# Where head outputs, norms and modulation stand in a two-block transformer kernel with hand-written engine programs

## Time and profile before

| | us |
|---|---|
| runs | 2436.47, 2440.69, 2446.38 |
| median of the runs | 2440.69 |
| profiled execution | 2446.27 |
| its span | 2444.5 |
| TensorE matmuls, busy | 1869.2 (76%) |
| TensorE weight loads, busy | 1217.9 (50%) |
| VectorE, busy | 813.5 (33%) |
| ScalarE, busy | 519.2 (21%) |
| GpSimd, busy | 87.7 (4%) |

### The profile page before, as it was taken

How to read it: one execution, slowest core, us unless ns; L and a number is a source line. 1 busy time by engine, 2 the same in 40 slices (tenths; PEclk the granted TensorE clock), 3 DMA queues, 4 the chain that set the end, 5 groups by cost and what they waited for, 6 DMA issues and landing times.

```text
span 2444.5 us, 28941 instructions
## 1 busy us (share of the span) xinstructions
PE 1869.2 (76%) x12708; PEld 1217.9 (50%) x12708; DVE 813.5 (33%) x1269; ACT 519.2 (21%) x776; POOL 87.7 (4%) x140
## 2 busy tenths in 40 slices
PE   7989999999998999787766666666566666666665
PEld 7879899988787998776321111211121211122111
DVE  5645567766455667554100110011001100110012
ACT  5625433345344343332000000000000000000000
POOL 1200000011000000010000000000000000000000
PEclk9999999999999999867977876888788877887886
DMA  7334557663345677324999999999999999999996
GB/s 242 96 127 150 179 175 258 207 193 121 121 138 164 207 249 240 122 112 198 390 429 429 429 429 428 429 429 429 429 429 430 429 429 429 428 429 428 430 429 265
DMA packets 171068, 739.79 MB, mean 303 GB/s; under 512 B 6672, under 2 KB 133136, under 8 KB 146240
## 3 DMA queue, kind: packets, MB, share of 16 engines
q1 hardware_dynamic: 168592, 731.27, 75.2%
q0 software_dynamic: 2352, 6.69, 0.8%
HBM read 736.88 MB, written 1.05 MB: 302 GB/s over the span
## 4 chain that ended last, share of the span: by engine, by line
DMA 47%; PE 40%; DVE 7%; ACT 4%; issue 2%; POOL 0%; SPq 0%; DVEq 0%; ACTq 0%
PE PS L325 39%; DMA WB<-in_w_down 24%; DMA WB<-in_w_up 23%; DVE WL L1430 2%; ACT WH L953 2%; DMA W<-in_w_in 1%; DVE X L1425 1%; DVE C L1425 1%; DVE S L1425 1%; DVE C L1422 0%; DMA W<-in_w_ck 0%; DVE S L1497 0%; DVE T L1422 0%; ACT S L983 0%; ACT C L1318 0%
## 5 line engine op out<-in xcount | busy, mean ns | idle before, releaser
L325 PE MATMUL PS<-WB,XS 128*32 128x352 f32 x3072 | 365.2, 637 | 210.1 <-DMA WB<-in_w_up 122.6
L325 PE MATMUL PS<-WB,S 128*32 128x512 f32 x1408 | 269.6, 762 | 152.1 <-issue 77.7
L1430 DVE TENSOR_TENSOR WL<-W,WH 128x2048 fp32r<-128x2048 f32 x141 | 323.4, 2294 | 169.0 <-ACT WH L953 169.0
L325 PEld LDWEIGHTS PS<-WB,XS 128*32 128x32 f32 x3072 | 115.9, 141 | 456.8 <-issue 178.9
L1425 DVE SCALAR_TENSOR_TENSOR S<-S,PS 128x352 f32<-128x352 f32 (+1 forms) x110 | 63.3, 588 | 792.9 <-ACT S L1395 756.2
L325 PE MATMUL PS<-HTh,WH 128*128 128x256 f32 x1064 | 307.0, 289 | 8.4 <-DVE WL L1430 4.7
L953 ACT ACTIVATE WH<-W 128x2048 fp32r<-128x2048 f32 x141 | 269.0, 1908 | 205.0 <-PE PS L325 190.6
L325 PE MATMUL PS<-HTl,WH 128*128 128x256 f32 x1064 | 302.4, 284 | 0.0
L325 PE MATMUL PS<-HTh,WL 128*128 128x256 f32 x1064 | 302.2, 284 | 0.0
L325 PEld LDWEIGHTS PS<-WB,S 128*32 128x32 f32 x1408 | 71.7, 128 | 339.7 <-issue 224.7
L325 PEld LDWEIGHTS PS<-HTh,WH 128*128 128x128 f32 x1064 | 205.0, 193 | 10.6 <-DVE WL L1430 5.2
(11 more groups left out here) (261 smaller groups left out, 2114.2 us busy)
## 6 DMA issues: line engine op xcount, KB each, us to landing
WB<-in_w_down SPq DMA_DIRECT2D x64, 2816.0 KB, 36.1
WB<-in_w_gate SPq DMA_DIRECT2D x48, 2816.0 KB, 35.9
WB<-in_w_up SPq DMA_DIRECT2D x48, 2816.0 KB, 35.9
C<-in_w_gate SPq DMA_DIRECT2D x16, 2816.0 KB, 36.5
C<-in_w_up SPq DMA_DIRECT2D x16, 2816.0 KB, 37.6
W<-in_w_in SPq DMA_DIRECT2D x31, 1024.0 KB, 6.7
S<-in_w_ada SPq DMA_DIRECT2D x24, 1024.0 KB, 5.3
W<-in_w_gate SPq DMA_DIRECT2D x22, 1024.0 KB, 7.9
```

The costliest lines, as they stand in the source:

```text
L325: return e.matmul(o, l, r, start=start, stop=stop, skip_group_check=True)
L1430: e.tensor_tensor(M.WL[i][:, :], M.W[:, 2048 * (m % NW):2048 * (m % NW) + 2048], M.WH[i][:, :].bitcast(F32), ALU.subtract).then_inc(*up("l ...
```

## The change

- **Head outputs**: scores are always in bank 0, transposed probabilities in bank 1, the output c in bank 2 + c % 2, with a signal `o_out` for its emptying; they draw no rotating bank. The first unit of `w_out` waits for each of the four banks as it comes to it (`of=("heads", l)`). `ret_s(0)` and `ret_s(1)` come before `heads(9)`, on VectorE `decayed(0)` and `decayed(1)` too.
- **Retention**: VectorE takes the first step of `retained()` (the sums) before the next unit's low part, not behind it. Six empty steps stand ahead of the split of the turned rows.
- **Modulation**: `modulation(12l)` is made in the cross attention, `modulation(12l + n + 1)` and `ada_sum(12l + n)` in slot n, the last sum before `down(10)`; the loads are put two slots earlier into the order of units.
- **Norms**: the squares are scaled by 1/32, so that the mean is one operation. VectorE scales the first half of the rows' columns, ScalarE the second, into `XN1` (exp: `XE`; mem, gm and at in place). TensorE turns by plain transposes. `pre_norm` turns all chunks of t = 0 before those of t = 1. A place with fewer than two fill units uses `pre_norm` behind them. exp's `XP` is made from `XE`, behind the evictions, by both engines. In a post-norm the first product comes ahead of the mean.

```diff
 
-    def turning(name, srcs, chunks, by=None, eighths=False):
-
+    def turning(name, srcs, chunks):
         for k0 in range(0, chunks, 2):
             ps = two(take(("turn", name, k0)))
             for k in range(2):
                 for t in range(2):
                     o, i = ps[:, k, 128 * t:128 * t + 128], srcs[t][:, 128 * (k0 + k):128 * (k0 + k) + 128]
-                    if eighths:
-                        i = srcs[t].rearrange("p (q k) -> p k q", k=8)[:, k0 + k, :]
-                    ins = e.transpose(o, i, M.ID) if by is None else mm(o, i, by[:, 128 * t:128 * t + 128], True, True)
+                    ins = e.transpose(o, i, M.ID)
             ins.then_inc(*up("full", "turn", name, k0))
             yield
 
...
-    def norming(name, src=X, dg=M.DG, eighths=False):
+    def norming(name, rows=M.XN1):
         yield
-        e.wait_ge(*at("diag", name))
-        yield from turning(name, [src[:, 0, :], src[:, 1, :]], 8, dg, eighths)
+        e.wait_ge(*at("scaled_first", name, 1))
+        e.wait_ge(*at("scaled_second", name, 1))
+        yield from turning(name, [rows[:, 0, :], rows[:, 1, :]], 8)
 
     def pre_norm(name, eighths=False):
-        for _ in norming(name, eighths=eighths):
-            pass
+
+
+        for t in range(2):
+            e.wait_ge(*at("scaled_first", name, t))
+            for k0 in range(0, 8, 2):
+                use = ("turn", name, k0)
+                if eighths or k0 == 4:
+                    e.wait_ge(*at("scaled_second", name, t))
+                if t == 0:
+                    take(use, hold=True)
+                ps = two(PS[:, 4 + C.banks.uses[use][0], :])
+                for k in range(k0, k0 + 2):
+                    i = M.XE[:, t, :].rearrange("p (q k) -> p k q", k=8)[:, k, :] if eighths else M.XN1[:, t, 128 * k:128 * k + 128]
+                    ins = e.transpose(ps[:, k - k0, 128 * t:128 * t + 128], i, M.ID)
+                if t:
+                    ins.then_inc(*up("full", *use))
+                    drop(use)
 
...
-        nrm = norming(name)
-        next(nrm)
         if len(units) < 2:
             for u in units:
                 fill(layer, *u)
-            for _ in nrm:
-                pass
+            pre_norm(name)
             return
+        nrm = norming(name)
+        next(nrm)
...
 
         def scores(h):
             c, po = h // 2, 64 * (h % 2)
-            ps = PS[:, h % 2, :]
-            if h >= 2:
-                e.wait_ge(*at("sc_out", l, h - 2))
+            ps = PS[:, 0, :]
...
 
         def values(h):
             c, po, Q = h // 2, 64 * (h % 2), M.PQ[h % 2]
-            ps = PS[:, 4 + C.banks.held[("o", l, c)], :] if h % 2 else take(("o", l, c), hold=True)
+            ps = PS[:, 2 + c % 2, :]
+            if h % 2 == 0 and c >= 2:
+                e.wait_ge(*at("o_out", l, c - 2))
+            elif h % 2 == 0 and l:
+                e.wait_ge(*at("yfree", "ffn", l - 1, 1, c))
             e.wait_ge(*at("pt_out", l, h))
             if h % 4 == 0:
                 e.wait_ge(*free("vv", l, h // 4))
             mm(ps[po:po + 64, 0:256], M.V[:, 0, 64 * h:64 * h + 64], Q[:, 0:256], True, False)
             mm(ps[po:po + 64, 128:256], M.V[:, 1, 64 * h:64 * h + 64], Q[:, 256:384], False, True).then_inc(*up("pv", l, h))
-            if h % 2:
...
             for _ in turning((w, l), [src[:, 0, :], src[:, 1, :]], 2):
                 pass
         fill(l, *f1)
-        heads(9)
         ret_s(0)
         ret_s(1)
+        heads(9)
         y = ("mix", l)
-        e.wait_ge(*free("o", l, 1))
-        for h in range(6, 8):
-            e.wait_ge(*at("sc_out", l, h))
-            e.wait_ge(*at("pt_out", l, h))
-        out_unit("w_out", l, 1, y, start=True)
+        e.wait_ge(*at("o_out", l, 1))
+        e.wait_ge(*at("sc_out", l, 7))
+        e.wait_ge(*at("pt_out", l, 7))
+        out_unit("w_out", l, 1, y, of=("heads", l), start=True)
         beside.finish(rec)
         psY = two(take(("ry", l), hold=True))
         ret_v(0)
         ret_v(1)
         ret_s(2)
         ret_s(3)
-        e.wait_ge(*free("o", l, 3))
+        e.wait_ge(*at("o_out", l, 3))
         out_unit("w_out", l, 2, y)
...
                 values(i - 2)
+            if i in (1, 2):
+                C.units.order.append(("ada", 12 * l + i - 1))
         e.wait_ge(*free("co", l, 2))
...
-            if n > 1:
-                ada_sum(12 * l + n - 2)
+            ada_sum(12 * l + n)
             proj_t("w_up", l, n, HT, ("u", l, n))
             if n > 1:
                 down(n - 2)
-            C.units.order.append(("ada", 12 * l + n))
+            if n < 10:
+                C.units.order.append(("ada", 12 * l + n + 2))
         down(9)
-        ada_sum(12 * l + 9)
+        ada_sum(12 * l + 11)
         down(10)
-        C.units.order.append(("ada", 12 * l + 11))
-        ada_sum(12 * l + 10)
-        ada_sum(12 * l + 11)
 
...
 
-    def squares(name, src, junk, ready):
+    def squares(name, src, ready):
         for t in range(2):
             for h in range(2):
                 e.wait_ge(*at(*ready, t, h))
-                e.activation(junk[t][:, 512 * h:512 * h + 512], src[:, t, 512 * h:512 * h + 512], ACT.Square,
+                e.activation(M.XN1[:, t, 512 * h:512 * h + 512], src[:, t, 512 * h:512 * h + 512], ACT.Square, scale=1.0 / 32,
                              accum_out=K["ss4"][:, 2 * t + h:2 * t + h + 1]).then_inc(*up("sq", name, t, h))
+
+    def scaled(name, src=X, dst=M.XN1):
+
+        for t in range(2):
+            e.wait_ge(*at("rstd", name, t))
+            e.activation(dst[:, t, 512:1024], src[:, t, 512:1024], ACT.Copy, scale=K["rs"][:, t:t + 1]).then_inc(
+                *up("scaled_second", name, t))
...
                 e.wait_ge(*at("pv", l, h - 2))
-            e.activation(M.PQ[h % 2][:, 0:384], PS[:, 2 + h % 2, 0:384], ACT.Copy).then_inc(*up("pt_out", l, h))
+            e.activation(M.PQ[h % 2][:, 0:384], PS[:, 1, 0:384], ACT.Copy).then_inc(*up("pt_out", l, h))
+            if h == 7:
+                C.sig.same(("yfree", "heads", l, 0, 1), ("pt_out", l, h))
 
...
             if h % 2:
                 e.wait_ge(*at("pv", l, h))
-                i, _ = C.banks.uses[("o", l, h // 2)]
-                e.activation(MX[0][:, 2 + h // 2, :], PS[:, 4 + i, 0:256], ACT.Copy).then_inc(*up("o_high", l, h // 2))
+                e.activation(MX[0][:, 2 + h // 2, :], PS[:, 2 + h // 2 % 2, 0:256], ACT.Copy).then_inc(*up("o_high", l, h // 2))
 
...
 
     e.wait_ge(*at("set"))
     e.activation(K["warm"], K["zero"], ACT.Square).then_inc(*step("act_step"))
-    nrm = norming(("mix", 0), par("pre_mix0", 0, 8), ("x",))
-    next(nrm)
+    squares(("mix", 0), X, ("x",))
+    scaled(("mix", 0))
     high(0)
...
-    squares(("exp",), X, M.NSQ, ("x", "mix2"))
-    for t in range(2):
-        e.wait_ge(*at("rstd", ("exp",), t))
-        e.activation(M.XP[0][:, t, :], X[:, t, :], ACT.Copy, scale=K["rs"][:, t:t + 1]).then_inc(*up("xp_high", t))
+    squares(("exp",), X, ("x", "mix2"))
+    scaled(("exp",), X, M.XE)
     for k0 in (2, 6):
         ps = two(full("turn", ("exp",), k0))
         for k in (k0, k0 + 1):
             ins = e.activation(M.HF[:, k, :], ps[:, k - k0, :], ACT.Identity, scale=K["gs"][:, 8 + k:9 + k],
                                bias=K["MT"][:, 16 + k:17 + k])
         ins.then_inc(*freed("turn", ("exp",), k0))
+    for t in range(2):
+        e.wait_ge(*at("scaled_first", ("exp",), t))
+        e.wait_ge(*at("scaled_second", ("exp",), t))
+        e.activation(M.XP[0][:, t, :], M.XE[:, t, :], ACT.Copy).then_inc(*up("xp_high", t))
...
-    def diagonal(name, dst, rs):
-
-        for t in range(2):
-            e.wait_ge(*at("rstd", name, t))
-        ts(dst[:, 0:128], M.ID, rs[:, 0:1], None, ALU.mult)
-        ts(dst[:, 128:256], M.ID, rs[:, 1:2], None, ALU.mult).then_inc(*up("diag", name))
-
     def mean_square(name, ready, t, out):
 
         e.wait_ge(*ready)
-        e.tensor_tensor(K["ms"][:, t:t + 1], K["ss4"][:, 2 * t:2 * t + 1], K["ss4"][:, 2 * t + 1:2 * t + 2], ALU.add).then_inc(*step())
-        own()
-        ts(K["ms"][:, t:t + 1], K["ms"][:, t:t + 1], 1.0 / 1024, EPS, ALU.mult, ALU.add).then_inc(*up(out, *name, t))
-
-    def norm_head(name, dg=M.DG):
+        stt(K["ms"][:, t:t + 1], K["ss4"][:, 2 * t:2 * t + 1], EPS, K["ss4"][:, 2 * t + 1:2 * t + 2], ALU.add, ALU.add).then_inc(
+            *up(out, *name, t))
+
+    def norm_head(name, src=X, dst=M.XN1):
+
         for t in range(2):
             mean_square((name,), at("sq", name, t, 1), t, "ms")
-        diagonal(name, dg, K["rs"])
+            e.wait_ge(*at("rstd", name, t))
+            ts(dst[:, t, 0:512], src[:, t, 0:512], K["rs"][:, t:t + 1], None, ALU.mult).then_inc(*up("scaled_first", name, t))
...
     def post_norm(y, gain, src=None, tmp=M.TMP):
         for t in range(2):
-            mean_square(y, at("ysq", *y, t, 1), t, "pms")
             for h in range(2):
+                if h:
```

(66 more changed lines are left out.)

37 lines of the change are left out of this document (20 added, 17 removed).

## The result

The changed kernel takes **2402.98 us** in the median (2399.49 to 2403.47, four runs) against 2443.53 for the kernel before in runs beside it (2436.47 to 2446.54): ratio 0.9835, 95% interval 0.9809 to 0.9861. Execution against execution, as the prediction's sum was made, it is 2446.3 to 2402.6 us: **43.7 us** won, where the sum said 50.6. The median came out 13 us above the forecast of 2390, inside the range. Some 7 of the 13 are the sum's. The other 6 are no term of it: the forecast took 5.6 off for the profiled execution before, which lay that far above its median, and the profiled execution after lies at its own.

A forecast was written before the change was run, and what follows sets the result against it. The end was taken as a constant (some 1,280 us of experts) after expert 0's inputs are ready, with TensorE's idle gaps before it. Terms summed to 50.6 us: 2395.7 from the profiled 2446.3, 2390 for the median; range 2373 to 2414.

The forecast's parts named there:

- Rival 5: The stream of weights sets the end by itself: no change, 2440 us; chance 0.04.
- Head outputs: Mixers, both layers: the waits of rq and ret_s(0) for a bank leave, with their half clock; 13.0 and 13.5 us won.
- retention sums: In each layer the retention's turning no longer waits 2.85 us for VectorE; 9.0 us won, clock included.
- mem: Memory norm: 1.9 us of TensorE won less 1.0 of waiting, 0.9 us won.
- The six yields: Split of the turned retention rows behind the next low part, ending just as out_unit(3) starts; 0 to 0.5 us lost.
- norms: Norms of the two layers: plain transposes take half the time of products with the diagonal; together 5.0 us won.
- clock given back: Half clock at new or longer pauses (gap at n = 0, shorter turnings at 767 and 985): -4 us, between 0 and 8.
- Modulation: Modulation made one slot earlier around the feed-forwards: 3.1 us won in layer 0, 6.4 in layer 1.
- exp: Experts' norm and router: 7.91 us of products become 4, router's products then run at 0.50; 3.8 us won.
- rival 2: Turning by transposes leaves the clock at 0.50 behind four exposed norms and the start: 2400 us; chance 0.17.
- rival 3: Another wait replaces the bank's: first w_out unit waits for o(3), or its low part is late; 2404 us; chance 0.12.
- Rival 1: The gaps go but the clock does not come back, so only idle time is won: 2410 us; chance 0.14.

The follow-up runs named there:

- Run 5: The changed kernel with the memory rows scaled wholly on VectorE, none on ScalarE: 2394.29 us, 8.3 faster than the changed kernel.
- Run 3: The changed kernel with GpSimd's wait ahead of the load of the post-norm's gain row (post_mix_g) removed: 2401.34 us, 1.3 faster than the changed kernel.
- run 7: The changed kernel with 24 unread transposes behind the first norm's turning, ahead of the first unit: 2399.51 us, 3.1 faster than the changed kernel.
- run 8: The changed kernel with 12 unread fp32 products (24 instructions) behind the first norm's turning, ahead of the first unit: 2402.76 us, 0.2 slower by the text.
- run 9: The changed kernel with the modulation's second half behind the hidden rows' low part in slots 0 and 1 of each feed-forward: 2404.8 us, 2.2 slower.
- run 11: The changed kernel with the early load of post_mix_g, memory rows scaled on VectorE alone, and 44 unread transposes ahead of the first unit: 2392.2 us, ratio to before 0.979.
- run 6: The changed kernel with fp32 products with the identity in place of the norms' plain transposes: 2420.52 us, 17.9 slower than the changed kernel.
- run 12: The changed kernel with all mends of run 10 and run 11, plus unread transposes in three more TensorE waits: 2377.66 us, ratio to before 0.974.
- run 1: The kernel before with only the head outputs part of the change: 2414.33 us against 2438.91, ratio 0.9897.
- run 2: The changed kernel with the retention sums' first step put back behind the next unit's low part: 2408.36 us, 5.8 slower than the changed kernel.
- run 4: The changed kernel with one empty step in place of six ahead of the split of the turned retention rows: 2400.31 us, 2.3 faster.
- run 10: The changed kernel with the modulation order of run 9 and each load of w_ada one unit later: 2394.0 us, 8.6 faster than the changed kernel.

## Why the prediction was right, and where it wasn't

**The frame held.** The end follows the first expert's inputs one for one; the constant stayed. Rival 5 falls. The pause shrank from 17 to 12 us, since the last load into the big buffers was released 37 us earlier and the first expert 42.6: so some 12 us of cover are left for gains that don't reach that load.

**Head outputs** (26.5) and **retention sums** (9.0) were right in place, mechanism and size, by an experiment each. "What is late next" was rightly put at nothing for the head outputs.

**mem was mis-sized, and its sign:** +0.9 predicted, -4.0 measured. The step says "1.9 of TensorE less 1.0 of waiting". It counts VectorE's and GpSimd's chain and forgets that ScalarE has a share now, whose job in the lane is stepped behind a high part and a head's exponentials: the power of t = 1 was there at 79.0 us, and ScalarE came to the scaling at 82.33. Run 5 gives back 5.8 at the place.

**The six yields:** "it then ends just as out_unit(3) starts (bound: 0 to 0.5 lost)". I asked only who waits for the split on TensorE. GpSimd waits too: behind its wait stands the load of the gain row, and behind that the post-norm, the low part, the fill. Run 3 measures it as 2.9 and 1.2 at the places, 4.1 of the 7.4 that the norms' row is short of its 5.0. The bound was drawn without one reader of the signal.

**The norms' other shortfall is the clock.** At the second layer's feed-forward norm 2.5 us were won up to the first product (1.8 forecast) and 2.8 lost behind it. 1.6 of these are half clock; the other 1.2 are the sum of w_ada that now stands behind this unit (16 products from 748.73), so they belong to the modulation, as does a like step of 0.35 in layer 0. That the shorter turning leaves less time in which the clock comes back is an argument and not shown: in five runs with the same turning and the same gap the half clock was not there (runs 5, 7, 8, 9 and 11). The -4 for "clock given back" was meant for this, but it had to serve the modulation too.

**Modulation** came to 7.0 where terms and give-back made 5.5; with the two sums just named it is 5.5, and the norms' row is -0.9, of whose shortfall the late load (4.1) and the half clock (1.6) explain all but 0.2. Layer 0's seam won 7.1, but the gap ahead of u1 grew by 1.5 (as forecast, 1.84 with what stands by it) and took the clock: 3.6 and 3.7 lost in the two layers. In layer 1 the loop, for which I had +0.7, won 1.7, and the half clock behind the gap of the earlier trace rows left with 1.5.

**exp** won 5.6 against 3.8. The terms that have a number there make only 2.8 (3.9 + 0.9 - 1.0 - 1.0); the 1.0 that is missing can only be XP's, which got none. That a transpose is half of a product was right and larger than I had it (run 6), and the router's products do run at 0.50 throughout, 1.3 us longer, as the step said.

**Rivals 2 and 3**, whose 2400 and 2404 lie nearer to the result than 2390, are refuted as mechanisms (runs 11 and 12, and run 1). But half clock behind the start and behind exposed norms, which rival 2 named, is there in the changed kernel; what is refuted is that the transposes keep it low. **Rival 1** came partly true: the clock isn't paid back gap by gap. Up to the first expert's first product, TensorE was busy at half clock for 111 us before and for 98 after. Half of the difference, some 6 us, was won by it, where the clock terms stood for 15.3 less 4.

Of the signs of being wrong, one came: the clock is at 0.50 in the first unit, and from 192 to 195 and 315 to 318 us, where it was 1.00 in the same work before. That the sum came as near as it did is in part luck: mem, the norms and the start fell short by 13.1 us together, and the other rows happened to bring 6.2 more than forecast, 1.1 of it inside the experts, where nothing was changed. The lower end of the range was also drawn too low; the parts named for it make 13.5 us, 2376 and not 2373.

## What to carry to other kernels

Two kernels with the same order of work are best compared unit by unit: the steps in the difference of start times add up to the result, and each has a place. When a step moves, list every engine that waits for its signal and what is queued behind that wait; here the costly readers were GpSimd's, with a DMA behind it, and SyncE's, with a load behind a load. When work is split over two engines to halve it, the half on the engine with the fuller queue sets the time: one operation of 0.75 us on the other beat two halves of 0.49 and 0.72.

## What the runs showed of the hardware

**Transposes hold the granted clock here.** 44 plain transposes and nothing else kept it at 1.00 for 5.6 us, and it stayed there for the unit behind (run 11); 36 did so in a wait in the middle (run 12). In run 9 the clock rose with nothing but transposes behind a long gap: the turning from 739.77 to 743.44 ran at 0.50, and the unit that started at 744.17 found it at 1.00. The Trainium skill (TensorE: Matmul & The Clock Gate, Part 4: PE-mode transpose) says that transposes don't count as busy TensorE work; no run here bears that out, and for these fp32 transposes the measurement decides.

```profile
739.77:743.44 3.67, 3.67 (x16) 3.27 (x16) 0.78 (x3) 2.14 (x6) 2.23 (x4) 0.50 0.26 105
744.20:750.20 6.00, 6.00 (x48) 5.84 (x48) 5.13 (x9) 1.03 (x3) 0.00 (x0) 1.00 0.39 156
```

**The same gap is not always followed by the same half clock.** The turning behind 5.68 us of idle time is the same code in changed and in run 9; the unit behind it took 7.66 us in one and about 6.0 in the other. Of the ten traces that have this turning and this gap, the changed kernel and runs 2, 3, 4 and 10 are like the one, and runs 5, 7, 8, 9 and 11 like the other. So a gap has no fixed price: gains of one or two microseconds at a place can vanish in the total (run 3: 4.1 at the places, 1.3 in the sum), and several runs, or the places themselves, are needed to see them. What decides it between two such traces stays open.
